# Sample-token outputs of four recurrent mixers: tokens on partitions, heads in four column groups of TensorE

## The reference, cut to what matters

```python
num = einsum('bhts,bhse->bhte', qk, vh) + inter[..., None] * einsum('bhtd,bhde->bhte', qh, cm)
den = sum(qk, axis=-1) + inter * einsum('bhtd,bhd->bht', qh, nm)
hout = num / maximum(abs(den), exp(-m_t))[..., None]
```

## Time and profile before

| | |
|---|---|
| median of 3 runs | 1483.66 us |
| lowest, highest | 1474.27, 1489.93 us |
| the profiled execution: its own time, its span | 1486.53, 1484.7 us |
| mean granted clock of TensorE in it | 0.940 |
| PE busy, share of the span | 1405.7 us, 95% |
| DVE, ACT, POOL busy | 57%, 39%, 7% |

### The profile page before, as it was taken

The page is one execution under the profiler, slowest core; times in us unless marked ns, Lnnn a source line. Parts: engine busy times, 40 slices in busy tenths (PEclk is TensorE's granted clock), DMA queues, the critical chain, the costliest instruction groups (busy, mean ns, idle before and its releaser), DMA issues.

```text
span 1484.7 us, 28320 instructions
## 1 busy us (share of the span) xinstructions
PE 1405.7 (95%) x11576; PEld 1341.2 (90%) x11576; DVE 840.6 (57%) x1265; ACT 581.9 (39%) x837; POOL 108.6 (7%) x157
## 2 busy tenths in 40 slices
PE   5999998999999988999989999989999998999996
PEld 4999998999976988999989999989998788999995
DVE  4455546756435774554575554576573468455454
ACT  4333344553223442333453333446323325333342
POOL 5400000000020026000000000000000200300000
PEclk9999999999976889999999999999998868999998
DMA  7855444432311339554445554434222213854450
GB/s 210 175 169 170 163 156 135 131 121 92 101 33 32 94 113 186 169 162 160 133 143 170 170 166 159 157 114 142 86 91 82 44 35 102 172 171 159 153 171 32
DMA packets 205947, 193.85 MB, mean 131 GB/s; under 512 B 29380, under 2 KB 203924, under 8 KB 205728
## 3 DMA queue, kind: packets, MB, share of 16 engines
q1 hardware_dynamic: 200432, 184.50, 40.9%
q0 software_dynamic: 4496, 6.09, 2.8%
q10 hardware_dynamic: 928, 1.95, 0.4%
HBM read 186.32 MB, written 6.19 MB: 130 GB/s over the span
## 4 chain that ended last, share of the span: by engine, by line
PE 88%; DMA 5%; DVE 4%; ACT 2%; issue 1%; SPq 1%; ACTq 0%; DVEq 0%
PE ps L619 86%; DMA ring<-in_ffn_w_up 4%; PE ps L622 2%; DVE ring_r L1910 1%; DMA big<-in_x_prompt 1%; SPq L575 1%; DVE x L1978 1%; DVE y L1919 1%; ACT whigh_r L1468 1%; DVE y L1977 0%; DMA arena<-in_state_ret 0%; ACT lnr L1492 0%; ACT r2row L1493 0%; ACT hdn L1484 0%; ACT L1488 0%
## 5 line engine op out<-in xcount | busy, mean ns | idle before, releaser
L1910 DVE TENSOR_TENSOR ring_r<-ring,whigh_r 128x2048 fp32r<-128x2048 f32 (+1 forms) x166 | 371.5, 2239 | 357.3 <-ACT whigh_r L1468 357.2
L1468 ACT ACTIVATE whigh_r<-ring 128x2048 fp32r<-128x2048 f32 (+1 forms) x166 | 310.6, 1871 | 368.4 <-PE ps L619 335.4
L619 PE MATMUL ps<-hdn,ring_r 128*128 128x288 f32 x2016 | 333.8, 299 | 0.0
L619 PE MATMUL ps<-hdn,whigh_r 128*128 128x288 f32 x1888 | 304.8, 303 | 12.3 <-DVE ring_r L1910 12.3
L619 PEld LDWEIGHTS ps<-hdn,ring_r 128*128 128x128 f32 x2016 | 296.3, 193 | 0.3
L619 PEld LDWEIGHTS ps<-hdn,whigh_r 128*128 128x128 f32 x1888 | 270.7, 192 | 15.0 <-issue 13.4
L619 PE MATMUL ps<-y_r,whigh_r 128*128 128x288 f32 x1792 | 275.2, 297 | 0.0
L619 PEld LDWEIGHTS ps<-y_r,whigh_r 128*128 128x128 f32 x1792 | 252.1, 189 | 0.0
L619 PE MATMUL ps<-big_r,whigh_r 128*128 128x288 f32 x800 | 125.4, 298 | 0.0
L619 PEld LDWEIGHTS ps<-big_r,whigh_r 128*128 128x128 f32 x800 | 112.2, 188 | 0.7
L619 PE MATMUL ps<-arena_r,whigh_r 128*128 128x288 f32 x704 | 109.4, 296 | 0.0
(11 more groups left out here) (426 smaller groups left out, 1362.3 us busy)
## 6 DMA issues: line engine op xcount, KB each, us to landing
ring<-in_ffn_w_gate SPq DMA_DIRECT2D x44, 1024.0 KB, 5.3
ring<-in_ffn_w_up SPq DMA_DIRECT2D x44, 1024.0 KB, 5.4
ring<-in_ffn_w_down SPq DMA_DIRECT2D x32, 1024.0 KB, 5.0
ring<-in_w_in SPq DMA_DIRECT2D x30, 1024.0 KB, 5.2
ring<-in_ffn_w_down SPq DMA_DIRECT2D x16, 768.0 KB, 4.3
ring<-in_w_out SPq DMA_DIRECT2D x8, 1024.0 KB, 5.0
cst<-in_const POOLq DMA_DIRECT2D x1, 1953.5 KB, 10.2
big<-in_x_prompt ACTq DMA_DIRECT2D x2, 512.0 KB, 9.0
```

The costliest lines, as they stand in the source:

```text
L619: return pe.matmul(out, lhsT, rhs, start=start, stop=stop, **k)
L1468: A(high(pos)[:, 0:rows * 256], ring[:, s, 0:rows * 256], ACT.Copy)\
L1910: return TT(out, in_, high, ALU.subtract)
```

## The change

Sample outputs get two functions of their own on PE. `out_samples` puts the 32 tokens of head h on PSUM partitions 32h to 32h+31, with `QX` (32 columns) stationary and the state (64 columns, 65 for `ml`) moving, without the wait in the middle. ACT copies the 128x64 result into SBUF (`tokens_copy`, new tile `tokm`); for `ml` DVE divides it there with one column of denominators per token: the 65th column is the denominator, ACT takes its absolute value (`token_floors`), and the floors come as one column from four small products in `m_rows_back`. `samples_back` then turns each head back with a product against a 32x32 identity, into the same bank and place where the output stood before, with the `half_done` wait in its middle. `out` and `weights_sum` lose their sample branches, and so do `floors(2)` and `divided(2)`. Work is put in another order on PE, ACT and DVE: `samples_back` stands a little later than `out_samples`; the `ml` part begins with `weights_sum(0)`; on DVE the splits of the first two slots of `w_out` move behind `masked_queries` and behind `divided(1)`.

```diff
                 def m_rows_back(bank):
...
                     for h in range(H):
                         mm(ps[toks(h), bank, 386:387], mL[:, SEQ:T], ident[0:H, h:h + 1])
+                        mm(ps[toks(h), bank, 387:388], mR[:, SEQ:T], ident[0:H, h:h + 1])
...
+                def out_samples(m, bank):
+
+                    need("probs_ready", l, m, 2)
+                    need("qx_ready", l, m)
+                    if m != "ssd":
+                        states_in(l1, m)
+                    if m == "gdn":
+                        need("new_copied", l, 2)
+                    else:
+                        need("keys_read", l, m, 2)
+                    w = HW[m]
+                    for h in range(H):
+                        for bp in range(4):
+                            mm(ps[toks(h), bank, P:P + w], QX[m][:, h, bp, :], SX[m][:, bp, h, 0:w], bp == 0, False)
+                    for h in range(H):
+                        g = mm(ps[toks(h), bank, P:P + w], DT2[m][toks(h), :], V2[m][toks(h), 0:w], False, True)
+                    mark(g, "out_done", l, m, "tok")
+
+                def samples_back(m, bank):
+
+                    if m == "ml":
+                        need("raw_made", l, m, "tok")
+                    else:
+                        need("raw_copied", l, m, "tok")
+                    for t in range(2):
+                        for p in range(2):
+                            h = 2 * t + p
+                            g = mm(ps[rows(p), bank, t * NS:(t + 1) * NS], tokm[toks(h), TOKM[m], :], C("id32")[toks(h), :])
+                        if t == 0:
+                            mark(g, "half_done", l, m, 2)
+                            need("half_done", l, m, 2)
+                    mark(g, "out_done", l, m, 2)
...
-                out("ret", 2, 0)
+                out_samples("ret", 0)
                 after("decay_ready", "ssd", 2)
                 after("probs_ready", "ssd", 1)
                 scores2("ssd", 7)
                 after("new_copied", 2)
                 out("gdn", 1, 2)
+                samples_back("ret", 0)
...
-                out("gdn", 2, 2)
+                out_samples("gdn", 2)
                 after("state_first", "ssd")
                 out("ssd", 0, 6)
+                samples_back("gdn", 2)
...
-                out("ssd", 2, 6)
+                out_samples("ssd", 6)
                 after("sadd_read", "gdn")
                 state("ssd", 1, 0)
                 turn2("ml", 1)
+                samples_back("ssd", 6)
...
                 dups("ml", 0)
-                out("ml", 0, 3)
-                after("state_first", "ml")
                 after("sadd_read", "ssd")
                 weights_sum(0, 7)
+                out("ml", 0, 3)
+                out_samples("ml", 1)
+                after("state_first", "ml")
+                weights_sum(1, 6)
                 out("ml", 1, 4)
-                weights_sum(1, 6)
-                after("probs_ready", "ml", 2)
                 state("ml", 1, 5)
-                out("ml", 2, 1)
-                hold(sem("floor_ready"), l * 3 + 1)
-                weights_sum(2, 7)
+                samples_back("ml", 1)
                 slot_ready(l, POS_OUT)
...
                 after("raw_made", "ml", 1)
                 after("state_last", "ml")
                 sample_add("ml")
-                after("raw_made", "ml", 2)
                 sums("ml", (1, 7))
...
+                def tokens_copy(m, bank):
+                    need("out_done", l, m, "tok")
+                    mark(A(tokm[:, TOKM[m], :], ps[:, bank, P:P + HD], ACT.Copy), "raw_copied", l, m, "tok")
...
+                def token_floors(bank):
+                    need("out_done", l, "ml", "tok")
+                    A(cols[:, 9:10], ps[:, bank, P + HD:P + HE], ACT.Abs).then_inc(sem("floor_ready"), 1)
...
                 raw("gdn", 0, 3)
+                tokens_copy("ret", 0)
+                raw("gdn", 1, 2)
                 raw("ret", 2, 0)
                 square("ret")
-                raw("gdn", 1, 2)
                 first_state("ssd", 6)
                 snat_copy(0, 7)
+                tokens_copy("gdn", 2)
                 raw("gdn", 2, 2)
...
                 decay_exps("ml", 1, 5)
+                tokens_copy("ssd", 6)
                 mixed_high("ret")
...
                 floors(0, 7)
+                token_floors(1)
                 floors(1, 6)
                 act.wait_ge(sem("stored_ssd"), l1 * 64)
                 upper(l, POS_OUT + 1)
-                floors(2, 7)
                 square("ml")
...
+                def tokens_divided(bank):
+                    dve.wait_ge(sem("floor_ready"), l * 3 + 2)
+                    dve.wait_ge(sem("ml_exps"), l1)
+                    link(l, TT(cols[:, 9:10], cols[:, 9:10], cols[:, 8:9], ALU.max))
+                    link(l, dve.reciprocal(cols[:, 9:10], cols[:, 9:10]))
+                    mark(TS(tokm[:, TOKM["ml"], :], ps[:, bank, P:P + HD], cols[:, 9:10], None, ALU.mult), "raw_made", l, "ml", "tok")
+
+                def samples_divided(bank):
+                    need("out_done", l, "ml", 2)
+                    mark(CP(RAW["ml"][:, :, SEQ:T], B(bank, 2, NS)), "raw_made", l, "ml", 2)
...
                 decayed("ml")
-                lower_weights(l, POS_OUT)
                 split("gdn")
                 rooted("ssd")
                 masked_queries("ml", 0)
                 split("ssd")
+                lower_weights(l, POS_OUT)
+                divided(0, 3)
+                tokens_divided(1)
+                last_state("ml", 5)
+                samples_divided(1)
+                divided(1, 4)
                 lower_weights(l, POS_OUT + 1)
-                divided(0, 3)
-                last_state("ml", 5)
-                divided(1, 4)
-                divided(2, 1)
                 gated("ml")
```

More of the change, by code:

```diff
@@ L209 @@
     "kx_ready": "ret gdn ssd ml",
-    "half_done": "ret.2 gdn.2 ssd.1 ssd.2 ml.2 ml.den",
+    "half_done": "ret.2 gdn.2 ssd.1 ssd.2 ml.2",
     "samples_decayed": "ret gdn ssd ml",
@@ L368, in trunk_kernel @@
         tm2 = sb("Tms", [P, NS])
-        cols = sb("cols", [P, 8])
+        cols = sb("cols", [P, 10])
+        tokm = sb("tokm", [P, 2, HD])
+        TOKM = {"ret": 0, "gdn": 1, "ssd": 0, "ml": 1}
         pk = sb("pk", [NS, H, 8])
@@ L1113, in out @@
                     else:
-                        need("keys_read", l, m, 2 if c == 2 else 0)
-                        if m in ("ret", "ml") and c < 2:
+                        need("keys_read", l, m, 0)
+                        if m in ("ret", "ml"):
                             need("values_copied", l, m)
@@ L1130, in out @@
                                 mm(place[h], S1[m][rows(b), a, 0:HD], q, True, False)
-                            if c == 2:
-                                for bp in range(4):
-                                    mm(place[h], SX[m][:, bp, h, 0:HD], QX[m][:, h, bp, :], bp == 0, False)
                         for h, p in halves:
                             b, a = (h // 2, h % 2) if m == "ssd" else (h % 2, h // 2)
[L1136 to L1140, removed]
+                            g = mm(place[h], V[m][:, c, h, 0:HD], DT[m][:, b, c, a, :], c == 0, True)
+                        if t == 0 and m == "ssd" and c == 1:
                             mark(g, "half_done", l, m, c)
@@ L1154, in weights_sum @@
                                    True, False)
-                            if c == 2:
-                                for bp in range(4):
-                                    mm(place[h], SX["ml"][:, bp, h, HD:HE].broadcast_to([P, HD]), QX["ml"][:, h, bp, :],
-                                       bp == 0, False)
                         for h, p in halves:
-                            if c < 2:
-                                g = mm(place[h], ones[:, 0:HD], DT["ml"][:, p, c, t, :], c == 0, True)
-                            else:
-                                g = mm(place[h], ones[toks(h), 0:HD], DT2["ml"][toks(h), :], False, True)
-                        if c == 2 and t == 0:
-                            mark(g, "half_done", l, "ml", "den")
-                            need("half_done", l, "ml", "den")
+                            g = mm(place[h], ones[:, 0:HD], DT["ml"][:, p, c, t, :], c == 0, True)
                     for t in range(2):
@@ L1720, in square @@
                     else:
-                        need("raw_made", l, m, 2)
+                        need("raw_made", l, m, 1)
                     mark(A(SQ[m], RAW[m], ACT.Square), "out_squared", l, m)
@@ L2222, in m_tokens @@
                     TT(cols[:, 5:6], cols[:, 2:3], ps[:, bank, 386:387], ALU.subtract)
+                    CP(cols[:, 8:9], ps[:, bank, 387:388])
                     CP(sml[0:NS, 3, 0:H], mtk(2)[0:NS, 2, :]).then_inc(sem("m_tok_read"), 1)
@@ L2621, in _ @@
                 keys_spread("ret")
-                need("out_done", "ret", 2)
+                need("out_done", "ret", "tok")
                 decayed("ret")
```

(2 more changed lines are left out.)

20 lines of the change are left out of this document (6 added, 14 removed), and 3 rows, old and new, of the table ORDER.

## The result

The change took 1466.22 us (median of 4 runs, 1461.88 to 1471.40) beside 1482.69 for the kernel before (4 runs): a ratio of 0.9887, 95% interval 0.9845 to 0.9928. That is 16.5 us less. I had forecast 1477.0, with a range from 1468: too little by 10.8 us, and 1.8 us outside the range. The profiled execution took 1471.40 us (span 1469.6) against 1486.53: 15.13 less.

What follows compares the result with a forecast made beforehand. PE, busy 95% of the span, was taken to bound the kernel. 4.55 us less work minus a 1.2 us wait gives 3.35 a layer, 6.7 for two, from the 1483.66 median: 1477.0 us, range 1468 to 1487.

Steps and rivals of the forecast that it cites:

- Replaced: four sample outputs, 0: Sample outputs on PE: new form costs the same as the old, taken as 0, bounds 3.0 less to 1.1 more.
- the nearest operation's ratio of clocks (1.72): 32-column group at the lower clock: priced from the old form's slowdown, 1.72 times, giving 2.29 us.
- Removed: 4.79: `ml`'s tail on PE: dropping the sample tokens' denominators saves 4.79 us a layer, all on PE's path.
- Moves on DVE: Splits of `w_out`'s first two slots stand later on DVE: taken as 0, with 0.56 us as the bound.
- My fifth rival: The removed work was filling time another engine needed anyway, so nothing is gained: 1483.7 us, chance 3%.
- The new wait: PE before `sample_add("ml")`: DVE finishes `divided(1)` 3.1 us after `samples_back`, PE has 1.86 to do, waits 1.2.
- PE's own work, 4.55: PE's work per layer falls by 4.55 us: 4.79 removed, 0.24 added for the floors' column, 0 for replaced outputs.
- My fourth rival: The wait before `sample_add` keeps the clock low into the output projection: 17.4 us lost, 1494.4 in one layer, chance 5%.
- Second rival, side by side: 32-column products run in four column groups at once, up to four times as fast: 11.6 us more gained, 1465.4, chance 5%.
- Third rival, the clock in the middle: `ret`'s sample output to `ssd`'s second chunk: second layer's clock falls too, 1482.9 (12%), or first stays up, 1471.0 (7%).
- PE's instructions: Sign on PE: instruction count falls by 16 in two layers, per layer 48 removed and 32 + 8 added.

Runs made afterwards that it cites:

- three_new: The kernel before with the new sample-output form for `ret`, `gdn` and `ssd` only, `ml` left old: 1486.07 us, ratio 1.0011.
- no_den: The kernel before without the denominators and division of `ml`'s sample tokens, old products and order kept: 1486.88 us, ratio 1.0004.
- dve_order: The kernel before with only DVE's new order, the splits of `w_out`'s first two slots moved: 1485.89 us, ratio 0.9997.
- groups_in_turn: The change with two loops of `out_samples` swapped, so neighbouring products write different column groups: 1464.90 us, ratio 0.9888.
- before_again: The kernel before, unedited, profiled a second time: one run, 1479.15 us.
- ml_new: The change with the old sample outputs for `ret`, `gdn` and `ssd`, so only `ml` is new: 1473.57 us, ratio 0.9918.
- old_in_place: The change's order, but `ml`'s sample output in its old 64-column form at the new place, without the tokens' division: 1474.65 us, ratio 0.9934.
- chain_short: `filled` and `groups_in_turn` joined, with DVE's split of `w_out`'s second slot moved behind the split of `ml`: 1464.91 us, ratio 0.9875.
- filled: The change with `divided(1)` ahead of the samples' copy, and `gdn` and `ssd` output shares ahead of PE's wait: 1462.83 us, ratio 0.9859.

## Why the prediction was right in its parts and wrong in its sum

- *Replaced: four sample outputs, 0.* Right: 1.29, 0.25 and 0.70 (431.69 to 432.39) at the upper clock, 2.29 at the lower, and `three_new` at 1.0011. The price by the nearest operation's ratio of clocks (1.72) gave the lower one to the hundredth, with some luck: I multiplied 1.33 by 1.72, and the group went from 1.29 by 1.78.
- *Removed: 4.79.* Right for PE's work, and wrong as an argument. I took DVE's end, 0.45 ahead of PE's, for a margin; it was the signal's own delay (0.46 in the change, 478.98 to 479.44), and both chains ended together. `no_den` gives nothing, `dve_order` gives nothing, both together 7.2 us. *Moves on DVE* were priced at 0, and they are what lets the removal count. My fifth rival (3%) holds for the removal by itself.
- *The new wait.* The place and the chain were right: 3.3 us from the end of `samples_back` (476.15) to `sample_add` against 3.1 forecast. PE waited 1.77, not 1.2: behind the returned clock its cover took 1.02, not 1.86, and 0.50 of issue stood ahead of it.
- *PE's own work, 4.55.* **This is the step that failed.** It priced the whole tail at the lower clock, because the kernel before stayed there. From the start of `dups("ml")` to `out_part` the tail fell by 7.34 in the first layer (19.72 to 12.38), not by 4.55. Of that, `weights_sum(1)`, `out("ml", 1)` and `state` give 1.36, 1.12 and 0.16, the same products at the other level. My fourth rival asked whether the clock comes back later. It did fall in the new wait, but the end is as long as before (10.50 beside 10.51), since the kernel before was at the lower level there too. No case asked whether it comes back earlier, though the change put a new kind of product into the stretch.
- *Second rival, side by side:* not in the change, where the four products of one head stand together (40 ns each). `groups_in_turn` shows 18 ns. By the Trainium skill, TensorE: Matmul & The Clock Gate, Measured speedup vs the span model, three column tiles with 512 moving columns measured 2.38 times as fast; the 2.2 here, with four groups and 64 columns, agrees in kind. So the gain that I weighed is there in part, 2.2 times and not four, and only in an order of products that the row at 419.60 does not have.
- *Third rival, the clock in the middle:* the change has 34.00 and 34.02, once 31.05. The first layer's 38.15 recurs in `before_again`, `no_den` and `dve_order`, and in no kernel with the new products; but it is gone in `ml_new`, with the old ones, too. What parts 31 from 34 is the return behind `ssd`'s group. And `three_new` has the shorter first middle, and its ten runs show no gain. Whether the middle adds to the measured 16.5 stays open; the 12.54 of tails and ends lie within the interval of the ratio (10.7 to 23.0 us).
- *PE's instructions* fell by 8, not 16. I had counted 48 removed in a layer, with four products for the sample tokens' floors. They are two products, the 4 instructions of the row at 483.24. So 44 go and 40 come, in each of two layers.

## What to carry to other kernels

Where two engines end a stage within a signal's delay of each other, price a change on one as nothing until the other's chain is shortened as well. Price a stretch at the lower clock at both levels whenever the change puts other products into it: which level it runs at is part of what the change changes. And when products use separate column groups, let neighbours alternate between them.

## What the runs showed of the hardware that was not expected

A PE without idle time can stay at the lower clock: 6.56 of 6.56 us busy at 0.50 in `old_in_place`, behind 64-column products that move 32 columns each. Behind the 32-column form, which moves 65 columns each in the same stretch, it came back in 16 of 18 tails. Two returned late, in `ml_new` and `chain_short`, and behind `ssd`'s group of the same form, which moves 64 columns each, it came back at once in 6 of 18 places only. So the form favours the return and does not assure it; what else decides is open. In the change the clock fell again in a wait of 1.77 us (0.50 from 479.44 to 484.00); without the wait, in `filled`, `sample_add` took 1.12 in place of 1.98. In this kernel 32 instructions over four column groups took 1.29 us with the products of one group together, and 0.58 with neighbours in different groups.
